# One core, two transformer blocks: the memory is loaded first, tables come on ScalarE's queue, TensorE multiplies zeros until they land, keys stand ahead of modulation, and the result is stored in three parts

## The chip, the cores and the metric

One core of a Trainium2 chip runs one program. The metric is the device time of an execution in microseconds (us); three runs of the kernel before gave a median of 1791.81 us (1791.75 to 1792.29).

## What is computed

The reference runs a first block (two layers: modulated RMS norm, a mixer of Fourier, latent attention and convolution, a squared-ReLU MLP) on `x` and `ctx`, and on its result a second block (RWKV-7, S5 and gated linear attention in parallel, a cross attention to a memory, a gated convolutional FFN, a last RMS norm). All is float32; sequence, context and memory have 256 rows of 1024. The parts that the change touches:

```python
# modulation vectors of a layer, for x and for ctx
mx = split(silu(c) @ w_mod[l] + b_mod[l], 6)
mc = split(silu(c_ctx) @ w_mod[l] + b_mod[l], 6)
zx = modulate(rms_norm(x, norm1_g[l]), mx[0], mx[1]) @ w_in[l]
...
# second block: the memory is normed once, its keys and values serve the cross attention
mem_n = rms_norm_2(mem, norm_mem)
kv = mem_n @ xa_wkv            # 1024 x 2048: keys, then values
...
return rms_norm_2(x, norm_final)   # (1, 256, 1024)
```

## The kernel before

Activations lie transposed, features on the 128 partitions: a tensor of 1024 x 256 is 8 tiles of 128x256 (`KD` = 8, `T` = 256). All weights come as one stream of 128x128 tiles, 16 to a chunk of 1 MB; `weight_stream()` (line 130 on) writes their order, and TensorE's program must use them in the same order. The chunks go through a ring of four slots (`SLOTS`). SyncE (SP) issues their loads: chunks 0 to 3 at once (L2686), chunks 4 to 11 each after a wait that its slot's previous chunk is used (L2689), then `ctx`, `x` and the second part of the tables (L2690 to L2692), then all further chunks in a loop (L2697). TensorE announces a used chunk with its first product on the next one (`chunks_used`).

Each engine has its own hand-written program, and semaphores join them. A float32 product appears in the trace as two matmul instructions, all under line 681, the line of the helper `mm`. The start:

- SP issues, in this order: the first tables (ones, constants; L2680), the two `c` vectors (L2681), all small vectors (L2682), the memory in two halves of four tiles (L2684), then the ring. The first three count into `first_loaded`, and TensorE (L697), ScalarE (L1484) and VectorE (L2023) wait for all three before anything else.
- VectorE clears the small tile `cs` (in `raw`, L2122). ScalarE writes SiLU of `c` into it (L1498), loads the square root's table with a dummy activation (L1502), and squares the eight memory tiles (L1508), the fifth after `mem_loaded1`.
- TensorE sums the squares over the partitions by products with ones: 8 products of 128x128 by 128x256, into bank `mst`. ScalarE takes the root (L1511), VectorE the reciprocal (L2124) and scales each memory tile (L2126).
- TensorE meanwhile waits for `silu_c` and does modulation block 0 (`mod_block(0, 0)`: 8 products of 512 columns on quarter arrays, 32 tiles or 2 chunks), then keys 0 and 1 (`mem_keys(0, 2)`: 2 x 8 products of 256 columns, one chunk), block 1, keys 2 to 5, block 2, keys 6 and 7, the values' first half (2 chunks), the column sums of the squares of `x` and `ctx` (`("st", 0)`), block 3, and the values' second half with the turn of the modulation rows. ScalarE empties each key bank (L1515).

At the end VectorE scales the eight result tiles (L2674), each counting into `result`; SP waits for all eight, stores the result once (L2699) and waits for the store.

Of the kernel before, what the change touches and what calls it, by code (L numbers as in the profile page):

```python
# [24 lines left out]
ACT = mybir.ActivationFunctionType  # L25
AX = mybir.AxisListType.X

P = 128
T = 256
D = 1024  # L30
KD = D // P
# [32 lines left out]
CS_WIDE = 62  # L64
# [18 lines left out]
FY_STEP = (1, 2)  # L83
WF_STEP = (3, 4)

BRANCH_ORDER = [(n, b) for n in range(3) for b in (1, 2)] + [(n, 0) for n in range(3)]
# [43 lines left out]
def weight_stream():  # L130

    out = []
# [25 lines left out]
    def mod(l, q, k0=0, k1=KD):  # L158

        aligned()  # L160
        for k in range(k0, k1):
            for j in range(4):
                out.append((("mod", l, q, k, j), "w_mod", l, [(k * P, P, (4 * q + j) * P, P)]))

    def keys(n0, n1):
        for n in range(n0, n1):
            for k in range(KD):
                out.append((("xk", 0, n, k), "xa_wkv_2", 0, [(k * P, P, n * P, P)]))

    def values(half):  # L170
        for k in range(KD):
            for j in range(4):
                out.append((("xv", half, j, k), "xa_wkv_2", 0, [(k * P, P, D + (4 * half + j) * P, P)]))

    mod(0, 0)
    keys(0, 2)
    mod(0, 1)
    keys(2, 6)
    mod(0, 2)
# [135 lines left out]
NTAB_FIRST = sum(n for _, n in TABLES)  # L315
# [46 lines left out]
def two_blocks(nc, weights, ahead, vectors, table_in, x_in, ctx_in, mem_in, c_in, s5b_in, s5c_in, out):  # L362
# [3 lines left out]
    with ExitStack() as ctx:  # L366
        def sb(name, shape, dt=F32):
            return ctx.enter_context(nc.sbuf_tensor(name, shape, dt))
# [5 lines left out]
        xT = sb("xT", [P, KD, 2 * T])  # L374
# [55 lines left out]
        small2 = sb("small2", [P, 21, 16])  # L430
        sums = sb("sums", [P, 2, 3, 512])
        pend = sb("pend", [P, 4, NCH])
        gend = sb("gend", [P, 2, NCH])
# [128 lines left out]
        def fhid_form(f, kp):  # L562
# [13 lines left out]
                  "s5_gelu", "y_s5_ready", "rw_shifted", "rw_squash", "rw_dve", "rw_act", "y_rw_ready", "merged", "h2_raw", "both",  # L576
                  "pos_loaded", "ahead_norm2", "ahead_next", "ahead_last", "ahead_read", "square_sums", "rv_inverse", "h_half", "h_forms", "quad_sums", "first_product", "hid_forms", "x_next", "xmax", "xprob", "fconv", "fsilu", "fgate", "gains", "conv_first", "result", "h_scaled", "up_forms")
        S = {n: sem(n) for n in names}
# [7 lines left out]
        def taken(eng, key):  # L586

            b, n = plan[key]
            eng.wait_ge(bank_free[b], n)

        def bank(key):
            return ps[:, plan[key][0], :]
# [45 lines left out]
        def _(pe):  # L638
# [51 lines left out]
            def gemm(name, l, n, K, rhs, o_, key, m=P, ready=None):  # L690
                for k in range(K):
# [3 lines left out]
                    mm(o_, w[:, 0:m], rhs(k), k == 0, k == K - 1, key if k == K - 1 else None)  # L695

            pe.wait_ge(S["first_loaded"], 48)  # L697
            ones = table("ones")
# [89 lines left out]
            def mem_values(half, k0, k1):  # L788
# [4 lines left out]
                for k in range(k0, k1):  # L793
                    w = weight(("xv", half, 0, k), 4)
                    for tt in range(2):
                        mm(bank(("xv", half, tt)), memn[:, k, tt * P:(tt + 1) * P], w, k == 0, k == KD - 1,
                           ("xv", half, tt) if k == KD - 1 else None)

            pe.wait_ge(S["silu_c"], 2)
            mod_block(0, 0)  # L800
            mem_keys(0, 2)
            mod_block(0, 1)
            mem_keys(2, 6)
            mod_block(0, 2)
# [676 lines left out]
        def _(act):  # L1481
            did = signaller(act, "act_order")
            f = nc.scalar.activation
            act.wait_ge(S["first_loaded"], 48)  # L1484
            eps6 = table("eps6")
# [10 lines left out]

            act.wait_ge(S["silu_c"], 1)
            did(f(cs[:, :, CS_WIDE - 32:CS_WIDE - 30], cs_raw[:, :, :], ACT.Silu), "silu_c", wait=False)  # L1498

            def table_of(func):  # L1500

                did(f(warm[:, 0:1], eps6, func))  # L1502

            table_of(ACT.Sqrt)
            for k in range(KD):
                if k in (0, 4):
                    act.wait_ge(S[f"mem_loaded{k // 4}"], 16)
                did(f(memsq[:, k, :], memn[:, k, :], ACT.Square), "mem_squares", wait=False)  # L1508
            key = ("mst", 0)
            finished(act, key)  # L1510
            did(f(rinv2[:, 0:T], bank(key)[:, 0:T], ACT.Sqrt, bias=eps6, scale=1.0 / D), key=key)  # L1511
            for n in range(KD):
                key = ("xk", n)
                finished(act, key)
                did(f(first_k[:, n, :], bank(key)[:, 0:T], ACT.Copy), key=key, wait=False)  # L1515
# [504 lines left out]
        def _(dve):  # L2020
            did = signaller(dve, "dve_order")
            v = nc.vector
            dve.wait_ge(S["first_loaded"], 48)  # L2023
            def mods(l, part, n0, n1):
# [95 lines left out]

            quad_done = [0]
            did(v.memset(cs[:, :, :], 0.0), "silu_c")  # L2122
            taken(dve, ("mst", 0))
            did(v.reciprocal(rinv2[:, 0:T], rinv2[:, 0:T]))  # L2124
# [554 lines left out]
        def _(sp):  # L2679
            sp.dma_start(tab[:, 0:NTAB_FIRST], table_in[:, 0:NTAB_FIRST]).then_inc(S["first_loaded"], 16)  # L2680
            sp.dma_start(cs_raw[:, :, :], c_in).then_inc(S["first_loaded"], 16)  # L2681
            sp.dma_start(vec[:, :], vectors).then_inc(S["first_loaded"], 16)  # L2682
            for i in range(2):
# [10 lines left out]
            with sp.Fori(X_CHUNK // SLOTS, n_chunks // SLOTS) as i:  # L2694
                for c in range(SLOTS):
                    sp.wait_ge(chunks_used, i * SLOTS + (c - SLOTS + 1))
                    sp.dma_start(ring[:, c, :, :], weights[i * SLOTS + c, :, :, :]).then_inc(landed[c], 16)  # L2697
            sp.wait_ge(S["result"], KD)
            sp.dma_start(out, xT[:, :, T:2 * T]).then_inc(S["stored"], 16)  # L2699
            sp.wait_ge(S["stored"], 16)  # L2700

# [90 lines left out]
```

## Time and profile before

| | |
|---|---|
| median of 3 runs | 1791.81 us (1791.75 to 1792.29) |
| the profiled execution's own time | 1793.03 us |
| its span, first to last instruction | 1791.0 us |
| mean granted TensorE clock | 0.995 |
| busy: PE / PEld / DVE / ACT / POOL | 96% / 77% / 55% / 23% / 18% |
| chain that ended last, by engine | PE 84%, DVE 9%, ACT 2%, DMA 2% |
| DMA | 256.32 MB, mean 143 GB/s |

PE is TensorE's matmul rows, PEld its weight loads, DVE VectorE, ACT ScalarE, POOL GpSimd, SPq the queue of SyncE. Matmuls are pipelined, so a busy PE isn't at its peak. The granted clock (PEclk) is a share of 2.4 GHz: 1.00 is 2.4, 0.50 is 1.2 GHz. "us to landing" counts from the start of the issue to the semaphore. In a timeline row the first number is the start, the second the time in us, "x" the number of instructions merged, and in brackets stands the idle time of the engine before the first of them and what ended it.

### The profile page before, as it was taken

To read this page: it belongs to the slowest core of one execution; us is meant where nothing else is said; L and a number is where in the kernel's file an instruction comes from. 1 tells how busy PE (TensorE), PEld (TensorE's weight loads), DVE (VectorE), ACT (ScalarE), POOL (GpSimd) and SP (SyncE) were. 2 spreads that over 40 slices of the span, in tenths; PEclk is the share of its full clock that TensorE was granted. 3 is DMA by queue.
4 is the path that set the end of the run, shared out by engine and by line. 5 is a ranking of instruction groups with operands and counts; after the bars stand their busy time and mean duration, and the time that the engine had idled before them with its cause. 6 is when DMAs were issued, how large, how long until landed. Compare 5 with 4: busy or idle time off the path is not lost.

```text
span 1791.0 us, 27162 instructions
## 1 busy us (share of the span) xinstructions
PE 1721.3 (96%) x10938; PEld 1376.0 (77%) x10938; DVE 981.7 (55%) x1885; ACT 416.6 (23%) x807; POOL 321.8 (18%) x361
## 2 busy tenths in 40 slices
PE   7999999999999999999999999999999999999997
PEld 5434454488888888665799998877888788799996
DVE  1238562465676534577478754277831432288883
ACT  1312463321111210237322101323421101211110
POOL 0100172023001221005134201077000000001110
PEclk9999999999999999999999999999999999999999
DMA  7785333232333242330545554434222443344452
GB/s 276 299 321 200 118 118 145 71 121 91 118 119 117 94 168 91 118 118 25 216 161 168 170 176 170 141 118 142 95 73 72 158 148 118 116 147 162 165 184 99
DMA packets 38710, 256.32 MB, mean 143 GB/s; under 512 B 4128, under 2 KB 7328, under 8 KB 9024
## 3 DMA queue, kind: packets, MB, share of 16 engines
q1 hardware_dynamic: 34512, 228.29, 36.4%
q0 software_dynamic: 3504, 22.15, 3.2%
q10 hardware_dynamic: 576, 4.19, 0.6%
q8 instruction: 87, 1.43, 0.3%
q14 instruction: 31, 0.25, 0.0%
HBM read 247.28 MB, written 7.34 MB: 142 GB/s over the span
## 4 chain that ended last, share of the span: by engine, by line
PE 84%; DVE 9%; ACT 2%; DMA 2%; POOL 1%; issue 1%; SPq 0%; ACTq 0%; DVEq 0%; POOLq 0%
PE ps L681 83%; POOL aux L1948 1%; DMA ring<-weights 1%; PE ps L926 1%; DMA xT<-x_t 1%; DVE arena L2162 1%; DVE aux L2191 1%; DVE arena L2192 1%; DVE arena L2193 1%; ACT hT L1555 0%; POOL aux L1925 0%; DVE ring L2236 0%; DVE small L2204 0%; DVE aux L2095 0%; DVE aux L2100 0%
## 5 line engine op out<-in xcount | busy, mean ns | idle before, releaser
L681 PE MATMUL ps<-hT,ring 128*128 128x256 f32 (+3 forms) x3024 | 667.0, 381 | 8.0 <-ACT hT L1685 2.6
L681 PEld LDWEIGHTS ps<-hT,ring 128*128 128x128 f32 (+1 forms) x3024 | 514.2, 189 | 148.4 <-issue 88.2
L681 PE MATMUL ps<-arena,ring 128*128 128x256 f32 (+3 forms) x1884 | 355.4, 343 | 4.7 <-DVE arena L2193 3.4
L681 PEld LDWEIGHTS ps<-arena,ring 128*128 128x128 f32 (+1 forms) x1884 | 298.5, 191 | 50.9 <-issue 13.0
L681 PE MATMUL ps<-arena,sums 128*128 128x128 f32 (+1 forms) x966 | 161.6, 317 | 1.3 <-DVE aux L2262 1.3
L681 PEld LDWEIGHTS ps<-arena,sums 128*128 128x128 f32 x966 | 141.7, 191 | 12.3 <-DVE aux L2262 2.5
L1925 POOL TENSOR_TENSOR aux<-aux 128x256 f32<-128x256 f32 (+1 forms) x46 | 49.2, 1069 | 434.3 <-ACT aux L1490 365.3
L2235 DVE TENSOR_TENSOR sums<-ring 128x512 f32<-128x512 f32 x83 | 57.6, 695 | 65.0 <-PE ps L681 59.0
L681 PE MATMUL ps<-hT,sums 128*128 128x128 f32 (+1 forms) x592 | 89.2, 298 | 0.4 <-DVE aux L2262 0.4
L1969 POOL TENSOR_TENSOR arena<-arena 128x256 f32<-128x256 f32 (+1 forms) x32 | 26.4, 826 | 334.9 <-ACT arena L1679 334.9
L1948 POOL TENSOR_SCALAR aux<-aux,small 128x512 f32<-128x512 f32 (+1 forms) x48 | 70.9, 1486 | 81.2 <-DVE small L2211 80.7
L681 PEld LDWEIGHTS ps<-hT,sums 128*128 128x128 f32 x592 | 79.1, 192 | 4.7 <-DVE aux L2262 0.8
L1490 ACT ACTIVATE aux<-xT 128x256 f32<-128x256 f32 (+1 forms) x64 | 30.6, 492 | 218.5 <-DVE xT L2370 90.2
L1678 ACT ACTIVATE arena<-arena 128x1024 f32<-128x1024 f32 (+1 forms) x32 | 27.0, 844 | 215.1 <-DVE arena L2270 215.1
L2162 DVE SCALAR_TENSOR_TENSOR arena<-arena,vec 128x512 f32<-128x512 f32 (+1 forms) x120 | 73.7, 614 | 3.5
L2237 DVE TENSOR_TENSOR sums<-ring 128x512 f32<-128x512 f32 x83 | 67.4, 812 | 2.8
L681 PE MATMUL ps<-spare,ring 128*128 128x256 f32 x256 | 62.1, 386 | 2.5 <-DVE spare L2307 2.5
L2236 DVE TENSOR_TENSOR ring<-ring 128x512 f32<-128x512 f32 x83 | 62.1, 748 | 2.8
L2264 DVE TENSOR_TENSOR aux<-aux,ps 128x256 f32<-128x256 f32 x24 | 10.1, 421 | 97.0 <-PE ps L681 96.8
L2238 DVE TENSOR_TENSOR sums<-ring,sums 128x512 f32<-128x512 f32 x83 | 61.6, 743 | 2.8
L681 PE MATMUL ps<-spare,sums 128*128 128x256 f32 x256 | 58.1, 380 | 0.0
L681 PEld LDWEIGHTS ps<-spare,ring 128*128 128x128 f32 x256 | 49.4, 193 | 9.8 <-DVE spare L2307 2.9
(377 smaller groups left out, 1955.5 us busy)
## 6 DMA issues: line engine op xcount, KB each, us to landing
ring<-weights SPq DMA_DIRECT2D x212, 1024.0 KB, 4.9
arena<-ahead POOLq DMA_DIRECT2D x8, 1024.0 KB, 8.3
kept_turns<-aux ACTq DMA_DIRECT2D x4, 1024.0 KB, 5.7
arena<-kept_turns POOLq DMA_DIRECT2D x6, 512.0 KB, 6.3
kept_keys_values<-spare POOLq DMA_DIRECT2D x1, 2048.0 KB, 8.3
hT<-ahead POOLq DMA_DIRECT2D x2, 1024.0 KB, 6.3
spare<-ahead POOLq DMA_DIRECT2D x2, 1024.0 KB, 11.6
arena<-kept_keys_values POOLq DMA_DIRECT2D x1, 2048.0 KB, 8.6
```

The lines of the kernel that those rows point to most:

```text
L681: ins = nc.tensor.matmul(o_, lhsT, rhs, start=start, stop=stop, skip_group_check=True)
L926: ins = nc.tensor.transpose(o_[:, kt * P:(kt + 1) * P], prob[:, t % 4, kt * P:(kt + 1) * P], table("ident"))
L1490: did(f(sq[:, k, s], xT[:, k, s], ACT.Square), "squares", wait=False)
L1678: did(f(two, two, ACT.Relu))
L1925: did(nc.gpsimd.tensor_tensor(sq[:, 0, s], sq[:, 0, s], sq[:, k, s], ALU.add), "square_sums" if k == SUMMED[norm] - 1 else None)
L1948: did(nc.gpsimd.tensor_scalar(prob[:, t % 4, 0:nk], prob[:, t % 4, 0:nk], small[:, 3, t:t + 1], None, ALU.mult), "prob_ready", wait=False)
L1969: did(nc.gpsimd.tensor_tensor(t1, b12, b11, ALU.subtract))
L2162: did(v.scalar_tensor_tensor(dst, src, w, dst, ALU.mult, ALU.add), name)
L2235: did(tt(s3, a11, a21, ALU.subtract))
L2236: did(tt(a21, a21, a22, ALU.add))
L2237: did(tt(s2, a21, a11, ALU.subtract))
L2238: did(tt(s4, a12, s2, ALU.subtract), "quad_sums", wait=False)
```

## The change

- SP issues the memory's two halves and the ring first. The first tables, the vectors and `c` move to ScalarE's queue, ahead of ScalarE's other work.
- VectorE clears a 128x256 tile `zeros` (inside `sums`) and `cs` before it waits for `first_loaded`.
- TensorE does 5 products of zeros (into bank 4, which nobody reads then) before it waits for `first_loaded`, and 6 more between the column sums of the memory and the first key.
- ScalarE loads the square root's table with a dummy activation on `zeros` at its start and waits for `first_loaded` only before the root. SiLU, and the square root's table once more, come after the root.
- The weight stream and TensorE's program have keys 0 and 1, block 0, keys 2 and 3, block 1, keys 4 and 5, block 2, keys 6 and 7.
- The result is stored in parts of 3, 3 and 2 tiles, each as soon as its tiles are written.

```diff
+STILL = (5, 6)
+RESULT_PARTS = ((0, 3), (3, 6), (6, 8))
...
+    keys(0, 2)
     mod(0, 0)
-    keys(0, 2)
+    keys(2, 4)
     mod(0, 1)
-    keys(2, 6)
+    keys(4, 6)
     mod(0, 2)
     keys(6, 8)
...
+        zeros = sums[:, 0, 0, 0:T]
...
+            def still(count):
+                for _ in range(count):
+                    nc.tensor.matmul(ps[:, 4, 0:T], zeros[:, 0:P], zeros, start=True, stop=True, skip_group_check=True)
+
+            pe.wait_ge(S["zeros"], 1)
+            still(STILL[0])
             pe.wait_ge(S["first_loaded"], 48)
...
+            still(STILL[1])
+            mem_keys(0, 2)
             pe.wait_ge(S["silu_c"], 2)
             mod_block(0, 0)
-            mem_keys(0, 2)
+            mem_keys(2, 4)
             mod_block(0, 1)
-            mem_keys(2, 6)
+            mem_keys(4, 6)
             mod_block(0, 2)
...
-            act.wait_ge(S["first_loaded"], 48)
+            act.dma_start(tab[:, 0:NTAB_FIRST], table_in[:, 0:NTAB_FIRST]).then_inc(S["first_loaded"], 16)
+            act.dma_start(vec[:, :], vectors).then_inc(S["first_loaded"], 16)
+            act.dma_start(cs_raw[:, :, :], c_in).then_inc(S["first_loaded"], 16)
...
-            act.wait_ge(S["silu_c"], 1)
-            did(f(cs[:, :, CS_WIDE - 32:CS_WIDE - 30], cs_raw[:, :, :], ACT.Silu), "silu_c", wait=False)
...
-            table_of(ACT.Sqrt)
+            act.wait_ge(S["zeros"], 1)
+            table_of(ACT.Sqrt, zeros[:, 0:1])
             for k in range(KD):
                 if k in (0, 4):
                     act.wait_ge(S[f"mem_loaded{k // 4}"], 16)
                 did(f(memsq[:, k, :], memn[:, k, :], ACT.Square), "mem_squares", wait=False)
+            act.wait_ge(S["first_loaded"], 48)
             key = ("mst", 0)
             finished(act, key)
             did(f(rinv2[:, 0:T], bank(key)[:, 0:T], ACT.Sqrt, bias=eps6, scale=1.0 / D), key=key)
+            act.wait_ge(S["silu_c"], 1)
+            did(f(cs[:, :, CS_WIDE - 32:CS_WIDE - 30], cs_raw[:, :, :], ACT.Silu), "silu_c", wait=False)
+            table_of(ACT.Sqrt)
...
-            dve.wait_ge(S["first_loaded"], 48)
...
+            did(v.memset(zeros, 0.0), "zeros")
             did(v.memset(cs[:, :, :], 0.0), "silu_c")
+            dve.wait_ge(S["first_loaded"], 48)
...
-            sp.dma_start(tab[:, 0:NTAB_FIRST], table_in[:, 0:NTAB_FIRST]).then_inc(S["first_loaded"], 16)
-            sp.dma_start(cs_raw[:, :, :], c_in).then_inc(S["first_loaded"], 16)
-            sp.dma_start(vec[:, :], vectors).then_inc(S["first_loaded"], 16)
...
-            sp.wait_ge(S["result"], KD)
-            sp.dma_start(out, xT[:, :, T:2 * T]).then_inc(S["stored"], 16)
-            sp.wait_ge(S["stored"], 16)
+            for i, (a, b) in enumerate(RESULT_PARTS):
+                sp.wait_ge(S["result"], b)
+                sp.dma_start(out[:, a:b, :], xT[:, a:b, T:2 * T]).then_inc(S["stored"], 16)
+            sp.wait_ge(S["stored"], 16 * len(RESULT_PARTS))
```

## Rows read from the trace of the kernel before

**Rows 1.** The page, busy time of TensorE's matmul rows.

```profile
PE 1721.3 (96%) x10938; PEld 1376.0 (77%) x10938; DVE 981.7 (55%) x1885; ACT 416.6 (23%) x807; POOL 321.8 (18%) x361
```

**Rows 2.** The timeline of all engines, 0 to 28 us.

```profile
0.73 0.40 SPq L2680 DMA_DIRECT2D tab<-tables  x1
...
2.12 0.91 SPq L2684 DMA_DIRECT2D arena<-mem_t  x2
...
3.07 2.25 SPq L2686 DMA_DIRECT2D ring<-weights  x4
...
4.70 0.47 DVE L2122 MEMSET raw<- 128x496 f32 x1 [4.70 <-DMA vec<-vectors]
...
5.26 1.28 ACT L1498 ACT_TABLE_LOAD   x1 [5.26 <-DVE raw L2122]
...
6.79 1.28 ACT L1502 ACT_TABLE_LOAD   x1
...
8.31 2.56 ACT L1508 ACTIVATE arena<-arena 128x256 f32<-128x256 f32 x8
...
8.87 6.43 PE L681 MATMUL ps<-arena,tab 128*128 128x256 f32 x16 [8.87 <-ACT arena L1508]
...
15.23 1.92 PE L681 MATMUL ps<-ring,raw 128*32 128x512 f32 x16
...
18.25 7.17 PE L681 MATMUL ps<-arena,ring 128*128 128x256 f32 x32 [1.09 <-DVE arena L2126]
...
25.36 1.92 PE L681 MATMUL ps<-ring,raw 128*32 128x512 f32 x16
```

**Rows 3.** DMA issues, 2.0 to 2.5 us and 3.0 to 3.4: KB, us to landing.

```profile
arena<-mem_t SPq DMA_DIRECT2D x1, 512.0 KB, 5.5
...
vec<-vectors SPq DMA_DIRECT2D x1, 297.5 KB, 2.9
...
ring<-weights SPq DMA_DIRECT2D x1, 1024.0 KB, 8.5
...
arena<-mem_t SPq DMA_DIRECT2D x1, 512.0 KB, 6.6
```

**Rows 4.** TensorE: the sums, two waits, and the granted clock behind one.

```profile
L681 PE MATMUL ps<-arena,tab x13: 531/634/767, 8.9 to 14.1; 128*128 128x256 f32 x13
...
66.25 1.98 PE L681 MATMUL ps<-aux,tab 128*128 128x512 f32 x4 [2.27 <-POOL aux L1925]
...
355.42 3.49 PE L681 MATMUL ps<-spare,ring 128*128 128x256 f32 x8 [2.52 <-DVE spare L2307]
...
355.70:359.10 3.40, 3.40 (x9) 2.69 (x9) 3.33 (x3) 0.35 (x1) 0.00 (x0) 0.51 0.00 0
```

**Rows 5.** Keys 2 to 5, ring loads from 26 us, DMA rates (last column).

```profile
27.21 14.08 PE L681 MATMUL ps<-arena,ring 128*128 128x256 f32 x64
...
L2689 SPq DMA_DIRECT2D ring<-weights x6: 327/328/659, 26.4 to 43.2; - x6
...
DMA to landing us min/median/max: 4.8/6.3/9.7
...
ring<-weights SPq DMA_DIRECT2D x2, 1024.0 KB, 8.7
...
24.00:26.00 2.00, 2.00 (x15) 1.21 (x17) 0.00 (x0) 0.38 (x1) 0.00 (x0) 1.00 0.09 37
...
29.00:35.00 6.00, 6.00 (x29) 5.28 (x29) 0.00 (x0) 0.77 (x2) 0.00 (x0) 1.00 1.02 423
```

**Rows 6.** The end: timeline, landing of the store, DMA rate (last column).

```profile
1782.56 3.26 DVE L2674 SCALAR_TENSOR_TENSOR xT<-xT,vec,rinv 128x256 f32<-128x256 f32 x8
...
1785.85 0.61 SPq L2699 DMA_DIRECT2D result<-xT  x1
...
result<-xT SPq DMA_DIRECT2D x1, 1024.0 KB, 4.8
...
1788.00:1789.00 1.00, 0.00 (x0) 0.00 (x0) 0.00 (x0) 0.00 (x0) 0.00 (x0) 0.50 1.05 348
```

More of the change, by code:

```diff
@@ L576, in two_blocks @@
                   "s5_gelu", "y_s5_ready", "rw_shifted", "rw_squash", "rw_dve", "rw_act", "y_rw_ready", "merged", "h2_raw", "both",
-                  "pos_loaded", "ahead_norm2", "ahead_next", "ahead_last", "ahead_read", "square_sums", "rv_inverse", "h_half", "h_forms", "quad_sums", "first_product", "hid_forms", "x_next", "xmax", "xprob", "fconv", "fsilu", "fgate", "gains", "conv_first", "result", "h_scaled", "up_forms")
+                  "pos_loaded", "zeros", "ahead_norm2", "ahead_next", "ahead_last", "ahead_read", "square_sums", "rv_inverse", "h_half", "h_forms", "quad_sums", "first_product", "hid_forms", "x_next", "xmax", "xprob", "fconv", "fsilu", "fgate", "gains", "conv_first", "result", "h_scaled", "up_forms")
         S = {n: sem(n) for n in names}
@@ L1495, in root, with table_of @@
                 did(f(dst[:, s], bank(key)[:, s], ACT.Sqrt, bias=table(eps), scale=scale), key=key)
-            act.wait_ge(S["silu_c"], 1)
-            did(f(cs[:, :, CS_WIDE - 32:CS_WIDE - 30], cs_raw[:, :, :], ACT.Silu), "silu_c", wait=False)
-            def table_of(func):
-                did(f(warm[:, 0:1], eps6, func))
-            table_of(ACT.Sqrt)
+            def table_of(func, source=eps6):
+                did(f(warm[:, 0:1], source, func))
+            act.wait_ge(S["zeros"], 1)
+            table_of(ACT.Sqrt, zeros[:, 0:1])
             for k in range(KD):
```

## The prediction

> **What bounds the kernel now.** I read the page first: TensorE's matmul rows fill nearly all of the span [rows 1], so a microsecond is won only where TensorE stands still or runs slowly, or outside its work. The timeline of the first 28 us shows such a place. TensorE starts at 8.87 us, and its start is the end of a chain: the vectors land just before 4.70, VectorE clears the small tile at 4.70, ScalarE loads two tables of 1.28 us with a short activation behind each, squares the memory from 8.31 on, and the eight column sums of those squares (16 instructions) begin [rows 2, 3]. They end at 15.3; root (ScalarE), reciprocal and the first scaled memory tile (VectorE) follow, and the first key product starts at 18.25. Modulation block 0 (1.92 us) runs inside that last gap [rows 2]. From there TensorE is gapless to 64 us (the wait of 2.27 us before 66.25 is the next one [rows 4]), so whatever moves the first key product moves all that follows. The other place is the end: the last row is written by about 1785.8, and the result's single store takes 4.8 us to land [rows 6].
>
> A third loss is the clock. The granted clock's column has no lower value before the first recorded change, so I take the level from the durations: 13 of the 16 sum instructions take a median 634 ns and start about 0.43 us apart, against 0.22 for the same shape later (7.17 us for 32) [rows 2, 4]. So the engine, idle until 8.87, worked at 1.2 GHz until some 5.5 us later (13 x 0.43), then at 2.4.
>
> **Parts of the change, start of the kernel.** Loads: the memory's two halves go out at 0.73 and about 1.2 instead of 2.12 and 2.6, as three issues of 0.40 to 0.47 us leave SP's queue; ring chunk 0 goes out at about 1.65 instead of 3.07 [rows 2]. The three table loads pass to ScalarE's queue, from 0.73 to about 1.9 at SP's issue price; ScalarE has nothing else to do then. Now the two memory halves land at 7.6 (2.12 + 5.5) and about 9.2 [rows 3]. In the new order the first half can't beat 3.6 (0.73 plus the 2.9 us of the smaller vector load), and shouldn't be later than 7.6; I take 5.5. The second half is between 6.2 (the same spacing of 1.6 as now behind a first half at 4.6) and 9.2; I take 7.4, nearest to today's less the 1.4 of earlier issue. Tables are between 4.6 as now and 7.6, when today's tables and first half together are in; I take the middle, 6.1, because both queues use the same 16 engines.
>
> The Trainium skill (DMA: Bandwidth & Descriptors, Queues, rings and completion order) says that each DMA engine takes turns between the queues that have work, packet by packet. By that rule the tables, now unopposed, would be held back by the memory, and "memory first" is only half true; without it they would land at 4.6, the sums could start at 5.4, and the forecast would be 0.8 us lower. No row of this trace has two hardware queues busy together.
>
> ScalarE: its first table load needs only VectorE's zeros (its fill lies between nothing and the 0.47 us of the larger clear [rows 2]), so from about 2.0 to 3.3, ahead of the memory. SiLU and two table loads (about 3 us) move behind the root. They cost nothing: from the root's end at 10.6 they run to 13.6, and ScalarE's next task, to empty the first key tile, comes 16 products or 3.5 us after 13.05, while modulation block 0, which needs SiLU, comes at 20. Without that cover they would cost up to 3 us. VectorE's wait for the tables moves behind its clears and holds up only the reciprocal. TensorE: five zero products are ten instructions of 0.43 = 4.3 us, from 1.1 to 5.4, hidden as it would wait to 6.2 for tables. If those count like real work for the clock, it rises at 1.1 + 5.5 = 6.6, after one slow sum instruction. Sums: 6.2 + 15 x 0.22 + 0.2 for the slow one + 0.4 for the last one's tail = 10.1, instead of 15.3. They need memory's second half by 7.7, which I have. Behind them stands the same chain of 2.95 us (15.3 to 18.25), now filled with six zero products, 12 x 0.22 = 2.6 us, just under it. That matters: elsewhere an idle stretch of 2.52 us was followed by a granted clock of 0.51, with eight instructions taking 3.49 us, about twice their time [rows 4]; the wait of 2.27 at 66.25 [rows 4] had no such sequel. First key product: 10.1 + 2.95 = 13.05, **5.2 us earlier**.
>
> **The order of keys and modulation.** Modulation block 0 leaves the gap that hid it and stands in TensorE's gapless stretch: 27.21 - 25.36 = **1.85 us back** [rows 2, 5]. The order also asks more of the ring. A key chunk holds TensorE 7.0 us (64 instructions in 14.0 for two), a modulation block's two chunks only 1.85. Before, at the tightest place two key chunks followed one block; now every key chunk is followed by a block, so three chunks are wanted in 8.9 us. The nearest case: after the key chunk's end at 25.36 SP issued three loads, the first at 26.4 and the last of them after 27.6; two that were under way between 27.6 and 28 landed after a median 8.7, the slowest of all after 9.7, which I give to the third [rows 5]. Taken as issued at 27.7, it landed 12.05 after the chunk's end. The same three are issued after keys 0 and 1, at 20.15, and the third (keys 4 and 5) is wanted after block, keys, block: 1.85 + 7.05 + 1.85 = 10.75. So TensorE waits **1.3 us**; bounds are 0, if they land like the median load of that stretch (6.3 us [rows 5]), and 1.6, if the third was issued at 28.0. Later triples start while the queue is still running and should be in time. Chunk 0 is wanted at 13.05 and lands at latest at 11.6 as now (3.07 + 8.5 [rows 3]).
>
> The activations x are loaded behind chunk 11, which SP may send once chunk 7 is used, in the middle of modulation block 2 in both orders; so x comes earlier by what TensorE has won, and the wait of 2.27 us for its square sums [rows 4] stays. I cost it at nothing.
>
> **The stores.** SP waits for results 3, 6 and 8. They are ready 0.41 us apart from 1783.0 [rows 6], so at 1783.85, 1785.05 and 1785.85. A store's bytes start about 1.25 us after its issue (4.8 less 3.05 for 1 MB at 348 GB/s less 0.5 of tail) [rows 6]. First part: 1785.1 to 1786.25; second 1786.3 to 1787.45; third, 256 KB, 1787.45 to 1788.2, landed at 1788.75 instead of 1790.65: **1.9 us**. Bounds: 1.2, if each part brings 0.4 us of its own, and 2.3, if only the third's bytes count. The Trainium skill (same page, Anatomy of one DMA) fits a DMA by 2.0 us plus its bytes at 436 GB/s, on the path that GpSimd issues. An estimate by that page puts a 256 KB store at 2.6 us and so the gain at 2.2; the whole store would be 4.4 by it and the trace has 4.8 [rows 6], so my sum goes by the trace.
>
> **The sum:** 5.2 - 1.85 - 1.3 + 1.9 = 3.95 us. The profiled execution took 1793.03 us around a span of 1791.0, so it would become 1789.1 with a span of 1787.05. The median of the runs, 1791.81, stands 1.2 us lower; it becomes 1787.9.
>
> **Rivals.**
> A. *The ring keeps up.* No wait before keys 4 and 5: 1786.6. For it: the wait is half of one load's time, and the median load landed in 6.3 [rows 5]. Against: the 9.7 of just such a triple.
> B. *The zeros don't lift the clock, or the pause from 5.4 to 6.2 spoils it*, so that this part doesn't do what it says. The clock then rises 5.5 us after 6.2; 13 sum instructions run slowly, they end at 12.6, and 2.5 us of the gain are gone: 1790.4. For it: nothing here shows zero products; against: the rise came in the middle of like products, so it followed TensorE's work and not a change of work.
> C. *The memory's second half lands at 8.9 to 9.2, as now*, because the start-up of the 16 engines and not the order sets it (7.4 was taken, 9.2 is today's [rows 3]). The sums end 1.5 later: 1789.4.
> D. *The ring falls behind twice*, at keys 4 and 5 and again at 6 and 7: 1789.2.
> E. *Slower.* The same mechanism, further on: chunks 6, 9 and the x load each come a whole chunk late (2.5 us, 1.05 MB at 423 GB/s [rows 5]), since every triple is sent only as slots come free and x stands behind the last. Price 3 x 2.5 = 7.5 us at three places against the 5.25 won without a ring wait: 1794.1. It decides from 5.25 us of ring waits up. Against it: before the triple the DMA engines were almost idle (37 GB/s from 24 to 26 us [rows 5]), and three chunks are 7.5 us, less than the 8.9 they have.
>
> **Chances.** Forecast 38, A 22, B 14, C 11, D 10, E 5 of 100. What a measurement can tell from no change is about 0.2%, 3.6 us here, so "faster" begins at 1788.2, close above my number: it takes all of A and 27 of the forecast's 38, 49 in all; slower by over 3.6 us needs E at its worst, 4; the rest, 47, is within. The range reaches from 1785.8 (A with the memory in a microsecond earlier, or the store at its bound) to 1790.6 (B); E and some of the low end are left out.
>
> **What would show it.** Right: sum instructions of about 380 ns from 6.2 on, first key product near 13, the third store landing near 1786.7 (1788.75 less the 2.05 won before it); a TensorE wait "DMA ring<-weights" of about 1.3 us near 31. Wrong: 634 ns sums (B), sums waiting for ScalarE's fifth square (C), a second ring wait near 40 (D), a wait on x's sums well over 2.27 (E), a granted clock near 0.5 between 13 and 20 us. My number is wrong in sign if the ring's waits together exceed 5.25 us.

## The result and the profile after

The changed kernel took 1797.06 us (median of 6 runs, 1796.03 to 1799.83), the kernel before 1791.8 (6 runs beside them): the ratio is 1.0027, with a 95% interval of 1.0016 to 1.0037. Forecast were 1787.9 and a range up to 1790.6. So the change made the kernel slower by about 0.3%, the side to which the prediction had given 4 in 100. The profiled execution took 1796.82 us, its span 1794.8, 3.8 us over the one before. The medians differ by 5.3; both lie in the interval (2.9 to 6.6 us).

The timeline of the changed kernel's first 75 us (the products stand under L685 now, the zero products under L704; "..." stands for rows left out):

```profile
0.73 0.88 SPq L2700 DMA_DIRECT2D arena<-mem_t  x2
...
1.66 0.45 ACTq L1499 DMA_DIRECT2D cs_raw<-c_t  x1
...
1.18 4.38 PE L704 MATMUL ps<-sums 128*128 128x256 f32 x10 [1.18 <-DVE sums L2139]
...
5.60 1.33 ACT L1522 ACTIVATE arena<-arena 128x256 f32<-128x256 f32 x4 [1.96 <-DMA arena<-mem_t]
...
10.66 6.05 PE L685 MATMUL ps<-arena,tab 128*128 128x256 f32 x16 [5.10 <-DMA cs_raw<-c_t]
...
16.54 2.75 PE L704 MATMUL ps<-sums 128*128 128x256 f32 x12
...
19.74 7.17 PE L685 MATMUL ps<-arena,ring 128*128 128x256 f32 x32 [0.45 <-DVE arena L2145]
...
38.88 7.14 PE L685 MATMUL ps<-arena,ring 128*128 128x256 f32 x32 [1.15 <-DMA ring<-weights]
...
70.95 1.99 PE L685 MATMUL ps<-aux,tab 128*128 128x512 f32 x4 [2.24 <-POOL aux L1943]
```

Against [rows 2]: the memory's squares now start at 5.60 instead of 8.31, but the column sums at 10.66 instead of 8.87, behind an idle time of 5.10 us that the load of `c` ended, and the first key product at 19.74 instead of 18.25. Block 0 comes behind the first keys, at 26.85. Keys 4 and 5 wait 1.15 us for the ring (38.88). The sums of x start at 70.95 instead of 66.25 [rows 4].

The DMA issues of the changed kernel, first those under way between 0.5 and 1.0 us, in the second fence those between 1.6 and 2.0 (KB, us to landing):

```profile
arena<-mem_t SPq DMA_DIRECT2D x1, 512.0 KB, 4.8
...
tab<-tables ACTq DMA_DIRECT2D x1, 90.5 KB, 4.9
```

```profile
ring<-weights SPq DMA_DIRECT2D x1, 1024.0 KB, 8.5
...
arena<-mem_t SPq DMA_DIRECT2D x1, 512.0 KB, 6.4
...
vec<-vectors ACTq DMA_DIRECT2D x1, 297.5 KB, 6.8
...
cs_raw<-c_t ACTq DMA_DIRECT2D x1, 8.0 KB, 9.0
```

Against [rows 3]: the halves of the memory land at 0.73 + 4.8 = 5.5 and 1.19 + 6.4 = 7.6. ScalarE's three loads land at 5.6, 8.0 and 1.66 + 9.0 = 10.66. The 8 KB of `c` took 9.0 us, longer than a megabyte of weights that SP issued at the same moment (8.5).

How they share the DMA engines is seen in the packets of each queue between 8 and 9 us (packets, MB, share of 16 engines; q1 is SP's queue, q10 ScalarE's):

```profile
q1 hardware_dynamic: 56, 0.40, 95.1%
...
q10 hardware_dynamic: 56, 0.00, 3.8%
```

The queues moved as many packets each, 56 and 56, as they do if they take turns packet by packet. But for a few small ones, a packet of the ring is a row of 8 KB and one of `c` a row of 64 bytes. All loads here have 128 rows, one for each partition (1024 KB and 8 KB, divided by 128). So a load of 64-byte rows needs as many turns as a load of 8 KB rows, and lands with it.

The granted clock (the third figure from the end, before the DMA share and GB/s) in two stretches of the changed kernel, then the durations of its zero products, then of its first sums (ns, minimum, median, maximum):

```profile
5.00:8.30 3.30, 0.56 (x2) 0.09 (x1) 0.00 (x0) 2.06 (x7) 0.00 (x0) 1.00 1.06 432
...
8.30:11.00 2.70, 0.34 (x1) 0.34 (x2) 0.00 (x0) 0.60 (x2) 0.00 (x0) 0.55 1.01 414
```

```profile
L704 PE MATMUL ps<-sums x10: 381/632/792, 1.2 to 5.2; 128*128 128x256 f32 x10
```

```profile
L685 PE MATMUL ps<-arena,tab x11: 542/635/793, 10.7 to 15.1; 128*128 128x256 f32 x11
```

The last of the zero products took 381 ns: TensorE had gone from 1.2 to 2.4 GHz by about 5 us. Idle from 5.6 on, it fell back (0.55 from 8.3 to 11), so the sums ran at 635 ns once more, as in [rows 4].

The end, timeline and landings of the changed kernel:

```profile
1788.19 3.26 DVE L2693 SCALAR_TENSOR_TENSOR xT<-xT,vec,rinv 128x256 f32<-128x256 f32 x8
...
1789.50 2.35 SPq L2716 DMA_DIRECT2D result<-xT  x3
```

```profile
result<-xT SPq DMA_DIRECT2D x2, 384.0 KB, 2.6
...
result<-xT SPq DMA_DIRECT2D x1, 256.0 KB, 2.9
```

VectorE's last rows start 5.63 us later than in [rows 6] (1788.19 against 1782.56) and the span is only 3.8 longer: the stores gave back 1.8. The last one landed in 2.9 us instead of 4.8.

**The account of the profiled execution:** first key product 1.49 later, block 0 in the gapless stretch 1.85 (28.70 - 26.85), ring wait 1.15, and 0.2 in the pace of the products around the wait: 4.7 at the sums of x. One ring wait of 0.36 us near 102 is gone: 4.3. Then come two stretches at half clock, at 827.5 and 1397.5, that the kernel before did not have, less one that it had at 1099.9 and this one has not: together 1.3. The stores are -1.8. In sum 3.8. The rows of the two stretches, and then the kernel before at about the place of the first, with its granted clock at 1.00:

```profile
827.50:830.90 3.40, 2.77 (x9) 2.44 (x10) 1.94 (x6) 2.54 (x6) 3.40 (x3) 0.54 0.00 0
...
1397.50:1400.90 3.40, 3.15 (x21) 2.67 (x22) 2.02 (x5) 0.00 (x0) 0.00 (x0) 0.54 0.00 0
```

```profile
823.20:826.60 3.40, 2.74 (x15) 2.14 (x16) 2.22 (x7) 2.91 (x7) 3.40 (x3) 1.00 0.00 0
```

### The profile page after: what moved, and what is told of

It is laid out like the page before. It is cut to its first block, busy times and chain, and to the rows that moved or that the text cites. A ratio compares the mean times of both kernels' runs of the same rounds, so it can differ in the third digit from the quotient of the medians.

```text
span 1794.8 us, 27212 instructions
## 1 busy us (share of the span) xinstructions
PE 1729.6 (96%) x10960; PEld 1384.5 (77%) x10960; DVE 981.8 (55%) x1886; ACT 418.3 (23%) x809; POOL 321.7 (18%) x361
## 3 DMA queue, kind: packets, MB, share of 16 engines
q8 instruction: 87, 1.43, 0.3%
## 4 chain that ended last, share of the span: by engine, by line
PE 84%; DVE 9%; ACT 2%; DMA 2%; POOL 1%; issue 1%; ACTq 0%; SPq 0%; DVEq 0%; POOLq 0%
PE ps L685 83%; POOL aux L1966 1%; DMA ring<-weights 1%; PE ps L939 1%; DMA xT<-x_t 1%; DVE arena L2181 1%; DVE aux L2210 1%; DVE arena L2211 1%; DVE arena L2212 1%; DMA cs_raw<-c_t 0%; ACT hT L1573 0%; POOL aux L1943 0%; DVE ring L2255 0%; DVE small L2223 0%; DVE aux L2116 0%
## 5 line engine op out<-in xcount | busy, mean ns | idle before, releaser
L685 PE MATMUL ps<-hT,ring 128*128 128x256 f32 (+3 forms) x3024 | 667.8, 381 | 7.7 <-ACT hT L1703 2.6
L685 PEld LDWEIGHTS ps<-hT,ring 128*128 128x128 f32 (+1 forms) x3024 | 515.8, 190 | 147.6 <-issue 87.7
L685 PE MATMUL ps<-arena,ring 128*128 128x256 f32 (+3 forms) x1884 | 355.7, 344 | 5.2 <-DVE arena L2212 3.4
L685 PEld LDWEIGHTS ps<-arena,ring 128*128 128x128 f32 (+1 forms) x1884 | 298.8, 191 | 51.3 <-issue 15.0
L685 PE MATMUL ps<-arena,sums 128*128 128x128 f32 (+1 forms) x966 | 161.6, 317 | 1.3 <-DVE aux L2281 1.3
L685 PEld LDWEIGHTS ps<-arena,sums 128*128 128x128 f32 x966 | 141.9, 191 | 12.1 <-DVE aux L2281 2.5
L685 PE MATMUL ps<-hT,sums 128*128 128x128 f32 (+1 forms) x592 | 89.3, 298 | 0.5 <-DVE aux L2281 0.5
L685 PEld LDWEIGHTS ps<-hT,sums 128*128 128x128 f32 x592 | 79.1, 192 | 4.6 <-DVE aux L2281 0.9
L685 PE MATMUL ps<-spare,ring 128*128 128x256 f32 x256 | 62.0, 386 | 2.5 <-DVE spare L2326 2.5
L685 PE MATMUL ps<-spare,sums 128*128 128x256 f32 x256 | 58.2, 381 | 0.0
L685 PEld LDWEIGHTS ps<-spare,ring 128*128 128x128 f32 x256 | 49.4, 193 | 9.7 <-DVE spare L2326 2.9
```

The lines of the kernel that those rows point to most:

```text
L685: ins = nc.tensor.matmul(o_, lhsT, rhs, start=start, stop=stop, skip_group_check=True)
```

## The experiments

Each of the twelve ran beside the kernel before, on the same chip. The first column of times is the median, the second that of the kernel before beside it; the last two are starts in the profiled execution.

| run | us | before | ratio (95%) | first key product | sums of x |
|---|---|---|---|---|---|
| kernel before | 1791.8 | | | 18.25 | 66.25 |
| changed | 1797.06 | 1791.8 | 1.0027 (1.0016 to 1.0037) | 19.74 | 70.95 |
| changed again | 1798.15 | 1792.36 | 1.0035 (1.0023 to 1.0047) | 19.67 | 70.12 |
| e1 tables first | 1792.01 | 1792.67 | 0.9997 (0.9986 to 1.0008) | 14.83 | 64.99 |
| e2 own waits | 1789.35 | 1792.67 | 0.9982 (0.9973 to 0.9991) | 13.01 | 65.18 |
| e3 no zeros | 1798.09 | 1792.67 | 1.0025 (1.0016 to 1.0034) | 19.67 | 74.33 |
| e4 order alone | 1797.97 | 1792.67 | 1.0029 (1.0019 to 1.0039) | 18.07 | 72.62 |
| e5 stores alone | 1790.53 | 1792.76 | 0.9986 (0.9977 to 0.9994) | 18.05 | 66.26 |
| e6 own waits, no first zeros | 1791.38 | 1792.76 | 0.9989 (0.9980 to 0.9997) | 15.63 | 67.36 |
| e7 old order, SiLU first | 1790.32 | 1792.76 | 0.9983 (0.9974 to 0.9991) | 17.16 | 65.41 |
| e8 c first | 1796.59 | 1792.76 | 1.0018 (1.0009 to 1.0026) | 19.32 | 70.92 |
| e9 ring held | 1794.22 | 1792.36 | 1.0011 (1.0002 to 1.0020) | 16.15 | 67.57 |
| e10 before, zeros and stores | 1790.15 | 1792.36 | 0.9987 (0.9977 to 0.9996) | 16.23 | 64.20 |
| e11 wide order, x early | 1792.34 | 1792.36 | 1.0005 (0.9996 to 1.0014) | 12.81 | 67.72 |

The theory: the shared wait for ScalarE's three loads, the last of which lands with the ring's first chunk, holds the sums to 10.66 and costs the clock; the order of keys costs block 0 and the ring wait on top. Rivals: the clock or the zeros alone are to blame; any last load is late; the order is harmless.

**The repeat.** The changed kernel unaltered.

> The changed kernel once more, unaltered, on the chip of this batch: between 4 and 6 us over the kernel before if the loss isn't an accident of one chip; first key product at 19.5 to 20 us and c landed between 10.4 and 10.9.

Measured: 1.0035, `c` landed and the sums began at 10.44, the first key product at 19.67. The loss isn't an accident of one chip. The ring wait was only 0.17 here (1.15 in the first profile), so this part of the loss varies. Its sums of x, behind an idle time of 2.45 us, ran at half clock (the granted clock was 0.53 from 70.0 to 73.6) and took 3.66 us instead of 1.99:

```profile
70.12 3.66 PE L685 MATMUL ps<-aux,tab 128*128 128x512 f32 x4 [2.45 <-POOL aux L1943]
```

**e1, the tables back at the head of SP's queue**, ahead of the memory.

```diff
+            sp.dma_start(tab[:, 0:NTAB_FIRST], ...).then_inc(S["first_loaded"], 16)
+            sp.dma_start(cs_raw[:, :, :], c_in).then_inc(S["first_loaded"], 16)
+            sp.dma_start(vec[:, :], vectors).then_inc(S["first_loaded"], 16)
...
-            act.dma_start(tab[:, 0:NTAB_FIRST], ...).then_inc(S["first_loaded"], 16)
-            act.dma_start(vec[:, :], vectors).then_inc(S["first_loaded"], 16)
-            act.dma_start(cs_raw[:, :, :], c_in).then_inc(S["first_loaded"], 16)
```

> The changed kernel with one part undone: the three table loads are again the first on SP's queue, ahead of the memory; ScalarE issues none. Theory (the sums wait for the last table load, which landed at 10.66 us because ScalarE's queue shared the engines with memory and ring): tables land by 4.6 us, the memory's halves at 7.6 and 9.2 as before the change, the sums start at about 8.1 instead of 10.66 and the first key product between 14.5 and 17.0 instead of 19.74, so about 3 to 5 us less than the changed kernel (1792 to 1794 against 1797.1). Rival (the sums' start is set by ScalarE or by the zeros, and the loss is the clock's): the first key product stays within 1 us of 19.7 and the time within 1 us of the changed kernel.

Its timeline, sums and first key product:

```profile
8.11 3.69 PE L685 MATMUL ps<-arena,tab 128*128 128x256 f32 x16 [2.29 <-ACT arena L1519]
...
14.83 7.17 PE L685 MATMUL ps<-arena,ring 128*128 128x256 f32 x32 [0.45 <-DVE arena L2142]
```

The ratio fell from 1.0027 to 0.9997; sums at 8.11 and first key product at 14.83 are the theory's. With the memory *behind* the tables the sums start 2.5 us earlier than with it ahead. The zeros also paid here: an idle time of 2.29 us behind them, and the sums took 3.69 us. It isn't told apart from the kernel before, though the first key product is 3.4 us earlier. Block 0 and the ring take all but 1.26 us back by the sums of x, and in the profiled execution two stretches at half clock (0.53 at 822.0 and at 1392.0, as in the changed kernel) take the rest: VectorE's last rows start at 1782.60, against 1782.56 [rows 6]. Only the stores' 1.8 us are left in its span (1789.2).

**e2, a wait for each load.**

```diff
-            act.dma_start(vec[:, :], vectors).then_inc(S["first_loaded"], 16)
-            act.dma_start(cs_raw[:, :, :], c_in).then_inc(S["first_loaded"], 16)
+            act.dma_start(vec[:, :], vectors).then_inc(S["vec_loaded"], 16)
+            act.dma_start(cs_raw[:, :, :], c_in).then_inc(S["c_loaded"], 16)
...
-            pe.wait_ge(S["first_loaded"], 48)
+            pe.wait_ge(S["first_loaded"], 16)
...
-            act.wait_ge(S["first_loaded"], 48)
+            act.wait_ge(S["first_loaded"], 16)
             act.wait_ge(S["silu_c"], 1)
+            act.wait_ge(S["vec_loaded"], 16)
+            act.wait_ge(S["c_loaded"], 16)
...
-            dve.wait_ge(S["first_loaded"], 48)
+            dve.wait_ge(S["first_loaded"], 16)
+            dve.wait_ge(S["vec_loaded"], 16)
```

> The changed kernel, each of the three loads on ScalarE's queue with a semaphore of its own: TensorE and the root wait for the tables alone, VectorE for the vectors too, SiLU for c. Theory: tables landed at 5.64 and the memory's halves at 5.5 and 7.6, so the sums start at about 6.1, end near 10, and the first key product starts near 13 instead of 19.74; the order still costs block 0 (1.86) and the ring wait (1.15). About 6.7 us less than the changed kernel: near 1790.4, 1 to 2 us under the kernel before. Rival (c is late because all is late; the engines are shared and something else binds next): first key product later than 16 us and less than 4 us won.

Its timeline of TensorE: sums, first key product, keys 4 and 5, keys 6 and 7, sums of x:

```profile
6.02 3.96 PE L685 MATMUL ps<-arena,tab 128*128 128x256 f32 x16 [0.20 <-ACT arena L1522]
...
13.01 7.17 PE L685 MATMUL ps<-arena,ring 128*128 128x256 f32 x32 [0.44 <-DVE arena L2148]
...
32.91 7.14 PE L685 MATMUL ps<-arena,ring 128*128 128x256 f32 x32 [1.46 <-DMA ring<-weights]
...
42.90 7.14 PE L685 MATMUL ps<-arena,ring 128*128 128x256 f32 x32 [1.00 <-DMA ring<-weights]
...
65.18 1.98 PE L685 MATMUL ps<-aux,tab 128*128 128x512 f32 x4 [1.41 <-POOL aux L1945]
```

Nothing but the waits differs from the changed kernel, and the first key product moved from 19.74 to 13.01; `c` still landed near 10.7, but nobody on the path waited for it. This is the larger of the two repairs in total time (0.9982, and under the kernel before), though e1 and e2 reach the sums of x together (64.99 and 65.18) and their intervals touch. The ring now shows how tight the alternation is: waits of 0.24, 1.46 and 1.00 us. With block 0 they are why 5.2 us won at the first key product are 1.1 at the sums of x.

**e8, c first on ScalarE's queue, the shared wait kept.**

```diff
+            act.dma_start(cs_raw[:, :, :], c_in).then_inc(S["first_loaded"], 16)
             act.dma_start(tab[:, 0:NTAB_FIRST], ...).then_inc(S["first_loaded"], 16)
             act.dma_start(vec[:, :], vectors).then_inc(S["first_loaded"], 16)
-            act.dma_start(cs_raw[:, :, :], c_in).then_inc(S["first_loaded"], 16)
```

> The changed kernel with one thing moved: c is the first and not the last of ScalarE's three loads; the shared wait for all three stays. Theory (being last in ScalarE's queue, behind the vectors and beside memory and ring, made c land at 10.66): now the vectors are last, they carry 2.4 KB a row and land at 8.4 to 9, so the sums start about 2 us earlier than 10.66 and the time falls by 1.5 to 2.5 us. Rival (whichever load is last lands when the engines have done the ring's first chunk, near 10.5): sums start within 0.5 us of 10.66, no change.

Its first sums in the timeline, the DMA issues under way between 1.67 and 2.1 us, and the packets of the two queues between 8 and 9 us:

```profile
10.69 5.59 PE L685 MATMUL ps<-arena,tab 128*128 128x256 f32 x16 [5.58 <-DMA vec<-vectors]
```

```profile
ring<-weights SPq DMA_DIRECT2D x1, 1024.0 KB, 8.8
...
vec<-vectors ACTq DMA_DIRECT2D x1, 297.5 KB, 9.0
```

```profile
q1 hardware_dynamic: 51, 0.34, 79.7%
...
q10 hardware_dynamic: 51, 0.11, 28.4%
```

The rival was right. Whatever is third on ScalarE's queue, 8 KB or 298, lands at 10.7. In the changed kernel and here each of ScalarE's loads lands 0.1 to 0.5 us after the SP load that was issued at the same moment: first with the first half of the memory, second with the second half, third with chunk 0. My theory of the small load at the end of a queue was too narrow: it is the place, and what stands at that place on the other queue. Here too the queues moved packet for packet, 51 and 51, now with rows of 2380 bytes beside the 8 KB.

**e9, the ring held back.**

```diff
...
+            sp.wait_ge(S["first_loaded"], 48)
             for c in range(SLOTS):
                 sp.dma_start(ring[:, c, :, :], weights[c, :, :, :]).then_inc(landed[c], 16)
```

> The changed kernel, with SP's first ring load held back until all three of ScalarE's loads have landed (the memory's halves still go first). Theory (ScalarE's last load lands with the ring's first chunk because the 16 engines share their turns between the two queues): without ring bytes beside them c and the vectors land by 7 to 8 us instead of 10.66, the sums start near 7.7 and the first key product near 14.5; chunk 0 lands near 12 and is no bound. About 4 to 5 us under the changed kernel, though the ring waits may grow by up to 2 us. Rival (the last load on ScalarE's queue is slow by itself, by its place and its small rows): it still lands at 10 or later, and the ring comes later too, so the time is the changed kernel's or worse.

Its DMA issue of `c` (between 1.67 and 2.1 us), and its timeline of TensorE:

```profile
cs_raw<-c_t ACTq DMA_DIRECT2D x1, 8.0 KB, 6.0
```

```profile
7.71 5.41 PE L685 MATMUL ps<-arena,tab 128*128 128x256 f32 x16 [2.56 <-DMA cs_raw<-c_t]
...
16.15 7.17 PE L685 MATMUL ps<-arena,ring 128*128 128x256 f32 x32 [0.45 <-DVE arena L2145]
```

With no weights beside it `c` landed in 6.0 us instead of 9.0, at 7.7. That shows the ring's loads as the cause. The gain, 3.6 us at the first key product, is smaller than expected because the zeros were 2.56 us past when the sums began, and the clock had gone: 5.41 us for the sums, where e1 after 2.29 us had 3.69. In total time it is 3.9 us under the repeat on the same chip, just below the 4 to 5 that I had expected.

**e3 and e6, without zeros.** e3: `STILL = (0, 0)` in the changed kernel; e6: `STILL = (0, 6)` in e2.

> The changed kernel without any zero product (neither the 5 nor the 6). Theory (the zeros lifted the clock, and the idle 5.1 us up to 10.66 lost it again, so they bought nothing): sums take 6 to 6.5 us as in the changed kernel, first key product within 0.5 us of 19.74 unless the gap of 2.95 us behind the sums lets the clock fall, which adds up to 1.7 us; time within -0.5 and +2 us of 1797.1. Rival (the zeros themselves cost, or they keep the clock for the sums in most runs): 1 us or more less, or 3 us or more over it.

> The kernel with a wait of its own for each of ScalarE's loads, without the first 5 zero products (the 6 behind the sums stay). Theory (the zeros help only where real work follows them closely): the sums start at 6.0 us cold, 0.43 us apart, take 5.6 to 6.2 us instead of 3.96, the first key product starts near 15 instead of 13.0, and the time is 1.5 to 2.3 us over the 1789.35 us of the kernel with them, less what the ring no longer has to be waited for. Rival (the clock is up for the sums anyway): the same within 0.5 us.

TensorE's timeline of e3, then of e6, sums and first key products:

```profile
10.68 5.95 PE L685 MATMUL ps<-arena,tab 128*128 128x256 f32 x16 [10.68 <-DMA cs_raw<-c_t]
...
19.67 10.04 PE L685 MATMUL ps<-arena,ring 128*128 128x256 f32 x32 [3.04 <-DVE arena L2145]
```

```profile
6.21 6.39 PE L685 MATMUL ps<-arena,tab 128*128 128x256 f32 x16 [6.21 <-ACT arena L1522]
...
15.63 7.17 PE L685 MATMUL ps<-arena,ring 128*128 128x256 f32 x32 [0.44 <-DVE arena L2148]
```

e3: the five zeros bought nothing in the changed kernel (sums at 10.68 and 5.95 us without them). The six behind the sums did: without them the engine stood 3.04 us, and the 32 key instructions took 10.04 us instead of 7.17, more than the 1.7 that I had allowed. e6: where the sums follow closely, the five zeros are worth 6.39 - 3.96 = 2.4 us of sums and 2.6 at the first key product. In the total time neither is told apart from its partner: e3's interval holds the changed kernel's ratio, though its sums of x start 3.4 us later, and e6's overlaps that of e2. Only the traces show it.

**e4, the order alone**, in the kernel before; the weight stream is changed in the same way.

```diff
+            mem_keys(0, 2)
             pe.wait_ge(S["silu_c"], 2)
             mod_block(0, 0)
-            mem_keys(0, 2)
+            mem_keys(2, 4)
             mod_block(0, 1)
-            mem_keys(2, 6)
+            mem_keys(4, 6)
...
```

> The kernel before with the new order of keys and modulation alone (in the weight stream and in TensorE's program). Theory: the gap of 2.95 us behind the sums is no longer filled, block 0 costs 1.86 us in the gapless stretch and keys 4 and 5 wait 1.0 to 1.5 us for the ring: 2.9 to 3.4 us over the kernel before (1794.7 to 1795.2), and up to 1.7 more where the clock falls in the empty gap. Rival (the order is harmless, the ring wait comes from the loads' start): at most 1.9 us over it.

Its timeline, the first keys and keys 4 and 5:

```profile
18.07 10.15 PE L682 MATMUL ps<-arena,ring 128*128 128x256 f32 x32 [2.95 <-DVE arena L2128]
...
40.46 7.14 PE L682 MATMUL ps<-arena,ring 128*128 128x256 f32 x32 [1.42 <-DMA ring<-weights]
```

1.0029: the order alone costs as much as the whole change. Its three parts are in the rows: block 0 (1.85), the ring wait (1.42), and a gap of 2.95 us with nothing in it, behind which the keys took 10.15 us instead of 7.17. I had allowed 1.7 us for that third part; it cost 3.0, so the loss of 5.3 us lies over my 2.9 to 5.1.

**e5, the stores alone**, in the kernel before.

```diff
-            sp.wait_ge(S["result"], KD)
-            sp.dma_start(out, xT[:, :, T:2 * T]).then_inc(S["stored"], 16)
-            sp.wait_ge(S["stored"], 16)
+            for a, b in ((0, 3), (3, 6), (6, 8)):
+                sp.wait_ge(S["result"], b)
+                sp.dma_start(out[:, a:b, :], xT[:, a:b, T:2 * T]).then_inc(S["stored"], 16)
+            sp.wait_ge(S["stored"], 48)
```

> The kernel before with the result stored in three parts alone. Theory: the last store (256 KB) lands about 2.9 us after its issue instead of 4.8, as in the changed kernel's trace, so the end behind the last VectorE row shrinks by 1.8 to 1.9 us; time about 1.9 us under the kernel before (0.1%). Rival (each store's fixed part eats it): 0.5 us or less won.

0.9986, or 2.2 us (median against median) with an interval of 1.1 to 4.1 us; the landings are those of the changed kernel (2.6, 2.6, 2.9). As the theory has it.

**e7, old order, SiLU first.** From the changed kernel: `mod_block(0, 0)` ahead of the keys and no zeros there, own waits as in e2, `c` first on ScalarE's queue, and SiLU with its table ahead of the square root's table and the squares (its diff is left out here).

> The changed kernel with the old order of keys and modulation (block 0 ahead of the keys, no 6 zeros), a wait of its own for each table load, c first on ScalarE's queue, and SiLU and its table ahead of the squares. Theory: c lands by about 4 us, SiLU and both tables are done by 6 to 7, the sums start at 6 to 7.3 and end at 10 to 11; block 0 then waits for ring chunk 1 (landed near 12.7) and the keys for chunk 2 (near 15), and behind them no ring wait follows. First key product at 14.5 to 15.5, which with block 0 already done is worth 3 us against the kernel before, and the stores 1.9: 4.5 to 5.5 us under it, about 1787 to 1788. Rival (c's small load is late again, or the ring's first chunks come later): 2 us or less under it.

Its timeline: SiLU's table, the sums, the first key product, the sums of x:

```profile
5.11 1.28 ACT L1516 ACT_TABLE_LOAD   x1 [5.11 <-DMA cs_raw<-c_t]
...
8.73 5.38 PE L684 MATMUL ps<-arena,tab 128*128 128x256 f32 x16 [3.04 <-ACT arena L1522]
...
17.16 7.17 PE L684 MATMUL ps<-arena,ring 128*128 128x256 f32 x32 [1.20 <-DVE arena L2144]
...
65.41 1.98 PE L684 MATMUL ps<-aux,tab 128*128 128x512 f32 x4 [2.52 <-POOL aux L1941]
```

Half wrong: `c` landed at 5.1, with the memory's first half, and not by 4; so ScalarE's tables came late and the squares at 8.17. The sums came 3.04 us behind the zeros and were slow again (5.38 us), and the first key product at 17.16 was about 2 us later than expected. No ring wait followed up to the values, and x's sums began 0.8 us earlier than in the kernel before. 0.9983 is about 3 us by the ratio (2.4 median against median), nearer to the rival's "2 us or less" than to the 4.5 to 5.5 of the theory, and mostly the stores.

**e10, the kernel before with zeros and stores.** Its loads and order unchanged; ten zero products ahead of `first_loaded`, both clears of VectorE ahead of its wait, three stores.

> The kernel before (its loads, its order) with two parts: ten zero products and VectorE's clears ahead of the table wait, and the three stores. Theory (zeros help where the sums follow within some 2 us): zeros run from 1.2 to 7.5 or 8.3, sums from 8.3 at the higher clock take 3.7 to 4 us instead of 6.4, block 0 fills the gap but may wait for chunk 1, the first key product starts at 15.5 to 16.5 instead of 18.25, no ring wait behind. With 1.9 for the stores 3.5 to 4.5 us under the kernel before. Rival (the ring's chunk 2 or x binds, or the clock falls all the same): 2.4 us or less.

Its timeline: the sums, the sums of x:

```profile
8.04 3.69 PE L682 MATMUL ps<-arena,tab 128*128 128x256 f32 x16 [0.40 <-ACT arena L1512]
...
64.20 1.98 PE L682 MATMUL ps<-aux,tab 128*128 128x512 f32 x4 [2.27 <-POOL aux L1929]
```

The sums ran at the higher clock (3.69 us), the second half of block 0 waited 0.92 us for chunk 1, and x's sums began at 64.20, the earliest of all. The span of its profiled execution is 4.0 us under the one before (1787.0), as the theory has it: 2.05 at the sums of x and the stores. The ratio of 0.9987 is only 2.3 us (interval 0.7 to 4.1), the rival's size; the traces kept don't show why the other executions gained less.

**e11, a wider order and x early.** e2 with keys 2 to 5 in one piece, block 2 behind keys 6 and 7, `X_CHUNK = 8`.

> The kernel with own waits (e2), its ring waits attacked: keys 0-1, block 0, keys 2-5, block 1, keys 6-7, block 2, and x, ctx and the tables' rest loaded behind chunk 7 instead of chunk 11. Theory (the alternation of one key chunk and one block outruns the ring, and x is late only by its place): no ring wait up to block 2, x's sums ready before TensorE wants them, so the column sums of x start near 61 us instead of 65.2 (e2) and 66.25 (before): 3 to 4.5 us under e2, about 1785 to 1786. Rival (x's 3.3 MB push chunks 8 and 9 back): a ring wait of 2 us or more at block 2 and nothing won.

Its timeline: the first half of block 2, and the sums of x:

```profile
46.98 1.07 PE L684 MATMUL ps<-ring,raw 128*32 128x512 f32 x8 [2.17 <-DMA ring<-weights]
...
67.72 1.88 PE L684 MATMUL ps<-aux,tab 128*128 128x512 f32 x4
```

The rival won. x was there in time, but its 3.3 MB stood ahead of chunks 8 to 10: ring waits of 2.17, 1.43 and 0.64 us, and a fallen clock on top (0.59 from 50 to 57 us). 1.0005.

## Why the prediction was wrong

By its own steps:

1. *Memory.* Taken 5.5 and 7.4, measured 5.5 and 7.6. Right.
2. *The tables at 6.1, within 4.6 and 7.6.* **This step failed.** It took the three loads as one and bounded them by what the memory's halves need. The first landed at 5.64, inside; but the wait is for all three, and the third landed at 10.66, beside the ring's first chunk, which my bound did not contain. SP's ring loads follow 0.9 us behind the memory's start, and I had written down that chunk 0 then goes out at 1.65, about the moment of the third ScalarE load. The rule that I quoted from the Trainium skill (DMA: Bandwidth & Descriptors, Queues, rings and completion order: the engines take turns between queues that have work) points this way, and the traces agree: the 90 KB of tables took 4.9 us instead of 1.9, `c` 9.0 beside the ring and 6.0 without it (e9), and the queues moved packet for packet (56 and 56; 51 and 51 in e8). What I had not drawn from it is that turns are counted in rows and not in bytes: the third load's 128 rows wait for the 128 of chunk 0. The same section says that a semaphore's increment is written only after every earlier write of that DMA engine, across its queues. That can have added to the end of the wait. It isn't the main part of it here, as packets of `c` were still moving with those of the ring between 8 and 9 us, and up to about 10. I priced sharing the engines at 0.8 us; the last of the three loads came 4.6 us later than the 6.1 taken for them all. My sentence that no row of the trace of before has two hardware queues busy together isn't right either: between 552 and 553 us SP's queue moved 32 packets and ScalarE's 30.
3. *Zeros and clock.* Right about what they do: they lift the clock near 5 us, and sums that follow closely take 3.96 us (e2). Wrong in this kernel only through step 2: rival B's pause was 5.1 us and not 0.8. The sums began 4.5 later than forecast (10.66 against 6.2) and took 2.1 longer than in e2 (6.05 against 3.96): nearly all of the 6.7 us between 19.74 and 13.05. In e2, with that one wait repaired, the first key product came at 13.01.
4. *The gap behind the sums* kept its length and its zeros: 16.7 to 19.74. Right, and more important than priced (e3, e4: 3 us of slow keys).
5. *Block 0* 1.85 forecast, 1.85 measured. *Ring wait* 1.3 forecast, 1.15 measured. That it came so near is partly luck: the wait before keys 4 and 5 was 0.17 in the repeat, nothing in e1 and 1.48 in e8, and in e2 the waits were 2.7 in three pieces, where rival D would have been right. *x's sums*: the wait of 2.27 stayed (2.24). Right.
6. *Stores* 1.9 forecast, 1.8 measured. Right. The estimate for the last store by the fit of the Trainium skill (DMA: Bandwidth & Descriptors, Anatomy of one DMA), 2.6 us, was too low: it took 2.9.

None of my rivals had the late tables: the slow side was sought in the ring. Rival C, the memory late, looked at the wrong queue. The sum with 19.74 in the place of 13.05 is +1.5 + 1.85 + 1.3 - 1.9 = +2.7; the profiled execution had +3.8, the rest mainly the clock's falls at 827 and 1397. Executions differ in where the clock falls: e5, whose start is that of the kernel before, had stretches at half clock at 822.7 and 1368.9 (0.52 and 0.51), and the kernel before had none there. So e2 shows the failed step, but only about half of the median's +5.3 (2.9 by the starts and the stores) is accounted for by the start of the kernel. Whether the changed kernel draws more falls later in its other executions stays open.

## What to carry to other kernels

Before small loads move to a second queue to make room for a large one, write beside each the load that the first queue issues at that moment, and compare their rows and not their bytes: with 128 rows each they landed together here, 8 KB and a megabyte alike. Let nobody on the path wait for a load that it doesn't read; one semaphore for each load was worth at least as much here (e2) as putting the loads back in order (e1). Work that sits in a gap was free here and kept the clock; moving it out cost its own time and slow products behind the empty gap (e4).

## What the runs showed of the hardware

An 8 KB load took 1.7 us on SP's queue ahead of the memory (e4); on ScalarE's queue it took 4.3 to 4.6 at the first place beside the memory (e7, e8), 9.0 at the third beside the ring and 6.0 at the third with the ring held (e9). Two hardware queues with work moved packet for packet, whatever the packets' size (8 KB beside 64 bytes, 56 and 56; 8 KB beside 2380 bytes, 51 and 51). Zero products lifted TensorE's clock: e2 with them had its sums in 3.96 us, e6 without them in 6.39. After them the clock stood through idle times of 0.20 (e2) and 2.29 us (e1) and was lost after 2.56 (e9), 3.04 (e7) and 5.10 (changed). The length of the idle time alone doesn't decide it: before the sums of x the clock was lost after 2.45 us in the repeat and stood after 2.48 (e5) and 2.52 (e7). An empty gap of 3.04 and 2.95 us ahead of the keys cost 2.9 and 3.0 us more in the 32 instructions behind it (e3, e4).
